# Roots and x2 loaded ahead of the first gathers, and a retimed steady schedule, in a one-core S5, conformer and PEER step

## The chip, the cores and the metric

One NeuronCore of a Trainium2 chip runs the whole kernel. The metric is the device time of the kernel in microseconds (us). Its engines are TensorE (PE), VectorE (DVE), ScalarE (ACT), GpSimd (POOL) and SyncE (SP); SP, ACT and POOL also issue DMAs. "PEq", "ACTq", "SPq" and "POOLq" in the profile are the sequencers of these engines.

## The reference, cut to what matters

There are 1024 prompt rows and 64 sample rows of width 1024, all in float32. Each row goes through a mixing layer and then through a PEER layer:

```python
def _layer(x, ...):
    xn = _rmsnorm(x, norm_mix)
    z = xn @ w_in                       # [u_ssm 512 | conv GLU input 1024 | gates 2048]
    y_ssm = S5(u_ssm)                   # diagonal complex state space
    branch_a = pa * sigmoid(qa)         # pa, qa = gelu(y_ssm) @ w_ssm_glu
    v = p * sigmoid(q)                  # conv GLU
    out = causal_depthwise_conv(v, width 31) + conv_b
    branch_b = silu(layernorm(out)) @ w_conv_out
    x = x + (sigmoid(g_A) * branch_a + sigmoid(g_B) * branch_b) @ w_out      # "x2"
    return x + peer(_rmsnorm(x, norm_ffn))

def block(xb):                          # PEER, 128 rows at a time
    q = (xb @ w_q).reshape(128, 8, 2, 128)
    v1, i1 = top_k(q[:, :, 0] @ keys1.T, 16);  v2, i2 = top_k(q[:, :, 1] @ keys2.T, 16)
    sc, pos = top_k(all sums v1 + v2, 16);     eidx = i1 * 128 + i2 at pos
    g = softmax(sc)
    act = gelu(sum(u_tab[eidx] * xb))   # one dot product per chosen expert
    return sum((g * act) * v_tab[eidx]) # 8 heads * 16 experts = 128 experts per row
```

A final RMSNorm follows. Every row picks its own 128 experts, so 8 KB (a row of u and of v) are fetched for each of 1088 x 128 choices: 1.14 GB.

## The kernel before, in words

**Two streams of work share the core.** The expert stream handles one tile of 128 rows at a time, 32 slots for each pair of heads. A slot is one gather of 128 expert rows (1 MB) into one of 8 ring buffers `rows` (POOL, line 1521), a dot product on DVE (line 1375), Gelu and the scaling of a diagonal matrix on ACT (lines 915 to 922), and two float32 products on PE that add the v rows into PSUM (line 760), after which the buffer is free again (`slot_free`). There are 1088 slots in 272 turns of 4 slots, so 64 turns for each group of two tiles. POOL issues the gathers of two turns ahead, as fast as buffers come free.

The mixing stream computes everything up to the scores of the PEER keys for one group of 272 rows (256 prompt, 16 sample) at a time; there are 4 groups. Its work is written out in half turns in two tables: `OPENING` for group 0 and `STEADY` for groups 1 to 3. The first dictionary of a table is the order of PE, the second that of the other engines; an entry `"cout": [68, 70, 72, 74]` puts the four pieces of this name into half turns 68, 70, 72 and 74. In `STEADY` ACT follows PE by one half turn (`lag` 1) where a piece is read from PSUM bank pair `ps_a`. The first `OPEN` (59) half turns of group 0 run alone. Then the turn loop starts. Turn t holds the half turns numbered 2t and 2t+1 of the mixing stream, called by `beside(number)`: on PE `beside(2t)`, two slots, `beside(2t+1)`, two slots. `mix_half` maps the number: the first 2 x `SKEW` (8) numbers finish group 0, and then 128 half turns of group 1 follow, and so on. So half turn 0 of a steady group lies at turns 4, 68 and 132, and half turn h lies h/2 turns behind it.

**The pieces that the change moves.** `xn` is 24 transposes on PE into 8 tiles of `ps_a` (2 banks), each copied out by ACT (`to_channels`, lines 599 and 800). `cq` is the first product behind it. `tap` is a unit of the depthwise convolution on DVE, four scalar_tensor_tensor instructions (line 1225); there are 32 units, the second 16 of them in half turns 31 to 46. `mean`, `centre`, `square`, `var`, `eps`, `root`, `scale` and `swish` are the layer norm behind the taps. `gate`, `glu`, `cout`, `out`, `q` are products of PE with 16 matmuls each (`out` has 6 more, which add x), and each reads one 512 KB slab of weights that SP loads into a ring of 4. `cout` on DVE (lines 1291 to 1296) forms `merged`, and PE's first `out` waits for all 8 of its parts (`merged_done`). `score` (line 698) goes to DRAM in `keep_scores` (ACT, lines 834 and 835) and `rows` (line 744) transposes x2 back into rows.

**Around the first gathers.** Each engine is an in-order queue. ACT stores x2 rows (`sq`, half turn 54) and inverse roots (`rs`, half turn 56) to DRAM. SP loads the scores of two heads back in half turns 54 and 56 (line 452), and in half turn 58 the x2 rows and the roots of tile 0 (`load_rows`, lines 461 and 462). DVE chooses the experts of the first pair behind its last opening half turn (`choose`, lines 1319 to 1351): `choose(0, 0)` and `choose(0, 1)` are the two key tops of head 0, `choose(0, 3)` gives its indices, on which POOL's first gather waits. ACT's `exps(0)` behind the opening needs the roots, DVE's `start(0)` (line 1389) needs x2 and roots, and each dot product comes after both.

## Time and profile before

| | us |
|---|---|
| median of 3 runs | 3489.51 |
| lowest, highest | 3487.99, 3494.52 |
| the profiled execution | 3491.98 |
| its span (first to last instruction) | 3489.9 |
| PE busy | 3148.8 (90%) |
| DVE busy | 2409.2 (69%) |
| POOL busy | 1417.6 (41%) |
| ACT busy | 1214.4 (35%) |

The span and all rows below are of the profiled execution. "DMA share" is the mean busy share of the 16 DMA engines in a stretch; it reads up to 1.02 where they never rest. A row of a timeline begins with start and duration in us from the start of the span; what stands in brackets is the idle time of the engine before it and what ended it. Times of matmuls are modelled at their ends.

### The profile page before, as it was taken

To read this page: it belongs to the slowest core of one execution; us is meant where nothing else is said; L and a number is where in the kernel's file an instruction comes from. 1 tells how busy PE (TensorE), PEld (TensorE's weight loads), DVE (VectorE), ACT (ScalarE), POOL (GpSimd) and SP (SyncE) were. 2 spreads that over 40 slices of the span, in tenths; PEclk is the share of its full clock that TensorE was granted. 3 is DMA by queue.
4 is the path that set the end of the run, shared out by engine and by line. 5 is a ranking of instruction groups with operands and counts; after the bars stand their busy time and mean duration, and the time that the engine had idled before them with its cause. 6 is when DMAs were issued, how large, how long until landed. Compare 5 with 4: busy or idle time off the path is not lost.

```text
span 3489.9 us, 33576 instructions
## 1 busy us (share of the span) xinstructions
PE 3148.8 (90%) x10016; PEld 1794.4 (51%) x10016; DVE 2409.2 (69%) x5463; ACT 1214.4 (35%) x4060; POOL 1417.6 (41%) x1240
## 2 busy tenths in 40 slices
PE   7998999999999999999999999999999777777776
PEld 6776555555655455555655555555555222322222
DVE  7824599776656699776656699777656666676674
ACT  4222443343333334343333343333333333333332
POOL 1201455433334355443334355343333444444443
PEclk9999999999999999999999999999999999999999
DMA  4257999999999999999999999999999999999998
GB/s 134 96 175 275 380 381 410 418 419 419 418 398 412 395 386 407 418 410 418 416 398 415 393 385 406 419 415 419 418 406 405 420 420 420 402 420 408 419 398 344
DMA packets 232069, 1336.40 MB, mean 383 GB/s; under 512 B 27664, under 2 KB 49296, under 8 KB 92624
## 3 DMA queue, kind: packets, MB, share of 16 engines
q0 software_dynamic: 156672, 1140.92, 79.7%
q1 hardware_dynamic: 62992, 179.96, 13.9%
q10 hardware_dynamic: 12224, 13.38, 1.1%
q8 instruction: 80, 1.31, 0.1%
q14 instruction: 101, 0.83, 0.1%
HBM read 1310.93 MB, written 23.23 MB: 382 GB/s over the span
## 4 chain that ended last, share of the span: by engine, by line
PE 53%; DMA 25%; DVE 10%; issue 5%; ACT 5%; POOL 2%; SPq 0%; POOLq 0%; DVEq 0%; ACTq 0%
PE ps_acc L760 29%; DMA rows<-in_experts,idx 24%; PE ps_a L596 13%; DVE rows L1375 4%; PE ps_a L671 4%; PE ps_v L596 3%; POOL rows L1521 2%; DVE va L1225 1%; PE ps_a L698 1%; ACT coef L918 1%; ACT uy L817 1%; ACT diag L922 1%; PE ps_y L638 1%; PE ps_a L675 1%; PE ps_v L682 0%
## 5 line engine op out<-in xcount | busy, mean ns | idle before, releaser
L760 PE MATMUL ps_acc<-rows,diag 128*128 128x512 f32 x4352 | 2020.8, 613 | 282.4 <-ACT diag L922 279.7
L1521 POOL DMA_INDIRECT rows<-in_experts,idx x1088 | 1280.1, 1177 | 1788.5 <-PE ps_acc L760 1468.6
L1375 DVE CUSTOM_DVE_ANT_0 rows<-rows,xn 128x1024 f32<-128x1024 f32 x1088 | 1328.4, 1232 | 839.1 <-DMA rows<-in_experts,idx 832.3
L760 PEld LDWEIGHTS ps_acc<-rows,diag 128*128 128x128 f32 x4352 | 824.3, 195 | 1335.4 <-issue 865.1
L915 ACT ACTIVATE act_v<-dots 128x2 f32<-128x2 f32 x544 | 110.6, 203 | 1894.1 <-DVE dots L1375 1891.1
L922 ACT ACTIVATE diag<-pk,coef 128x128 f32<-128x128 f32 x1088 | 377.2, 394 | 17.7
L596 PE MATMUL ps_a<-xnT,ring 128*128 128x272 f32 x1536 | 370.3, 396 | 0.9 <-ACT xnT L805 0.7
L596 PEld LDWEIGHTS ps_a<-xnT,ring 128*128 128x128 f32 x1536 | 293.4, 192 | 91.8 <-issue 34.8
L918 ACT ACTIVATE coef<-act_v,soft 128x1 f32<-128x1 f32 x1088 | 261.4, 287 | 17.9
L596 PE MATMUL ps_a<-gates,ring 128*128 128x272 f32 x1024 | 247.5, 395 | 15.2 <-ACT sig L892 14.4
L1225 DVE SCALAR_TENSOR_TENSOR va<-va,pk 128x302 f32<-128x302 f32 x480 | 250.2, 584 | 2.7
L596 PEld LDWEIGHTS ps_a<-gates,ring 128*128 128x128 f32 x1024 | 194.7, 191 | 78.2 <-issue 25.4
L671 PE MATMUL ps_a<-xnT,ring 128*128 128x272 f32 x512 | 130.3, 399 | 2.3 <-DVE xnT L1296 1.2
L596 PE MATMUL ps_v<-uy,ring 128*128 128x272 f32 x512 | 127.1, 398 | 2.5 <-ACT uy L873 2.5
L596 PEld LDWEIGHTS ps_v<-uy,ring 128*128 128x128 f32 x512 | 98.9, 193 | 28.6 <-issue 5.5
L671 PEld LDWEIGHTS ps_a<-xnT,ring 128*128 128x128 f32 x512 | 94.5, 190 | 31.1 <-issue 11.5
L1375 DVE DVE_READ_ACCUMULATOR2_ANT dots<- 128x1 f32 x1088 | 89.0, 82 | 0.0
L1493 POOL TENSOR_TENSOR rs<-rs,half 128x3 f32<-128x3 f32 x4 | 5.6, 1390 | 168.5 <-DVE rs L1172 168.4
L596 PE MATMUL ps_a<-uy,ring 128*128 128x272 f32 x256 | 65.9, 401 | 4.1 <-ACT uy L817 4.1
L596 PEld LDWEIGHTS ps_a<-uy,ring 128*128 128x128 f32 x256 | 49.6, 194 | 24.7 <-issue 11.5
L596 PE MATMUL ps_v<-xnT,ring 128*128 128x272 f32 x256 | 61.4, 393 | 0.0
L698 PE MATMUL ps_a<-pk,sig 128*128 128x128 f32 (+1 forms) x384 | 59.5, 275 | 0.0
(226 smaller groups left out, 2001.0 us busy)
## 6 DMA issues: line engine op xcount, KB each, us to landing
ring<-in_slabs SPq DMA_DIRECT2D x256, 512.0 KB, 7.8
rows<-in_experts,idx POOLq DMA_INDIRECT x1088, 12.6
ring<-made_slabs SPq DMA_DIRECT2D x24, 512.0 KB, 9.3
sc<-score_rows SPq DMA_DIRECT2D x68, 128.0 KB, 10.2
score_rows<-gp ACTq DMA_DIRECT2D x32, 256.0 KB, 9.6
xt<-in_x_prompt SPq DMA_DIRECT2D x4, 1024.0 KB, 13.1
x_rows<-xt ACTq DMA_DIRECT2D x4, 1024.0 KB, 12.3
x2t<-x_rows SPq DMA_DIRECT2D x8, 512.0 KB, 11.7
```

The source lines that it names most:

```text
L596: last = pe.matmul(out[:, 0:N], w, rhs[:, k, :], start=(k == 0), stop=(k == kt - 1))
L638: last = pe.matmul(out, w, hst[:, t % 2, c, i, 0:NK], start=False, stop=(c == 1))
L671: last = pe.matmul(out[:, 0:N], ring[:, slot, k * P:(k + 1) * P], merged[:, k, :], start=(k == 0), stop=(k == DT - 1))
L675: pe.matmul(out[:, n:n + width], xt[0:width, t, j * P:(j + 1) * P], eye2[0:width, 0:width], start=False, stop=False, skip_group_check=True)
L698: last = pe.matmul(out[0:width, t * KEYS:(t + 1) * KEYS], qT[:, m % 2, n:n + width], keys, start=True, stop=True)
L760: ins = pe.matmul(ps_acc[:, h, :], diag[:, slot, :], rows[:, slot, D + h * 512:D + (h + 1) * 512], start=first, stop=False, skip_group_che ...
L915: act.activation(act_v[:, cols], dots[:, cols], ACT.Gelu).then_inc(gelu_done, 1)
L918: act.activation(coef[:, s:s + 1], act_v[:, s:s + 1], ACT.Copy, scale=soft[:, n % 2, s:s + 1]).then_inc(coef_done, 1)
L922: act.activation(diag[:, s % RING, :], shape, ACT.Copy, scale=coef[:, s:s + 1]).then_inc(diag_done, 1)
L1225: last = dve.scalar_tensor_tensor(acc[:, c, :], src, wk, acc[:, c, :], ALU.mult, ALU.add)
L1375: ins = dve.tensor_tensor_reduce(rows[:, slot, 0:D], rows[:, slot, 0:D], xn[:, :], 1.0, 0.0, ALU.mult, ALU.add, dots[:, s:s + 1])
L1521: pool.indirect_dma_start(out=rows[:, slot, :], out_offset=None, in_=experts, in_offset=bass.IndirectOffsetOnAxis(ap=idx[:, a, k:k + 1], a ...
```

## The change

`OPEN` becomes 62 and `SKEW` 3: three more half turns of group 0 run ahead of the turn loop, two fewer lie inside it, and each steady group starts one turn earlier. In the opening SP loads scores one half turn earlier, x2 rows of tile 0 in half turn 55 and its roots in half turn 57, and DVE runs the first two `choose` steps at the head of its half turn 55, ahead of `ms2`. `xn` is cut into two parts of 4 tiles in half turns 0 and 1, and the first `cq` of a steady group goes from 1 to 2. Units 16 to 31 of the taps go to 31 + 3u/2 (31 to 53), the layer norm goes from 48..62 to 56..67, one gate from 54 to 69, `cout` on PE from 68..74 to 71..77 and on DVE from 70..76 to 73..79, and `out` from 77..91 to 78..92.

```diff
--- before.py
+++ after.py
@@ -64,7 +64,7 @@
 HALVES = 2 * TURNS
 PIECES = ("xn", "u", "cq", "cp", "s", "y", "gate", "glu", "mean", "var", "cout", "out", "rows", "q", "score")
 SLAB_OF = {"u": 0, "cq": S_CONV, "cp": S_CONV + 1, "gate": S_GATE, "glu": S_GLU, "cout": S_COUT, "out": S_OUT, "q": S_Q}
-A_TILES = {"xn": DT, "u": 1, "cq": 1, "gate": 1, "glu": 1, "out": 1, "q": 1, "score": 1}
+A_TILES = {"xn": DT // 2, "u": 1, "cq": 1, "gate": 1, "glu": 1, "out": 1, "q": 1, "score": 1}
 V_TILES = {"cp": 1, "s": 2, "glu": 1, "mean": 1, "var": 1, "cout": 2, "rows": 2}
 A_BANKS, V_BANKS = 2, 3
 
@@ -107,7 +107,7 @@
 
 
 OPENING = Plan(
-    {"xn": [0], "u": [1, 2, 3, 4], "cq": [5, 7, 9, 11], "cp": [6, 8, 10, 12],
+    {"xn": [0, 1], "u": [1, 2, 3, 4], "cq": [5, 7, 9, 11], "cp": [6, 8, 10, 12],
      "s": [10, 12, 14, 16], "y": [15, 18, 21, 24],
      "gate": [13 + m for m in range(13)] + [34 + m for m in range(3)], "glu": [26 + j for j in range(DT)],
      "mean": [29], "var": [32], "cout": [37, 38, 39, 40], "out": [42 + j for j in range(DT)],
@@ -120,27 +120,27 @@
      "cout": [38, 39, 40, 41], "rows": [52, 53, 54], "sq": [54], "ms2": [55], "rs": [56],
      "load_x": [59], "sq_next": [63], "ms_next": [64], "norm_next": [65]}, False, 0)
 STEADY = Plan(
-    {"xn": [0], "u": [9, 11, 21, 23], "cq": [1, 5, 13, 17], "cp": [3, 7, 15, 19],
+    {"xn": [0, 1], "u": [9, 11, 21, 23], "cq": [2, 5, 13, 17], "cp": [3, 7, 15, 19],
      "s": [12, 16, 24, 28], "y": [20, 24, 32, 36],
-     "gate": [25 + 2 * m for m in range(10)] + [44, 54] + [61 + 2 * m for m in range(4)],
+     "gate": [25 + 2 * m for m in range(10)] + [44] + [61 + 2 * m for m in range(5)],
      "glu": [45 + 2 * j for j in range(DT)],
-     "mean": [48], "var": [54], "cout": [68, 70, 72, 74], "out": [77 + 2 * j for j in range(DT)],
+     "mean": [56], "var": [61], "cout": [71, 73, 75, 77], "out": [78 + 2 * j for j in range(DT)],
      "rows": [94, 96, 98], "q": [93 + 2 * m for m in range(2 * HEADS)],
      "score": [95 + 2 * m for m in range(2 * HEADS)]},
     {"cp": [6, 10, 18, 22], "turn_in": [14, 18, 26, 30], "scan": [14, 18, 26, 30], "turn_back": [14, 18, 26, 30],
      "gelu": [21, 25, 33, 37],
-     "tap": [11, 12, 13, 15, 16, 17, 19, 20, 21, 22, 23, 24, 25, 27, 28, 29] + [31 + u for u in range(16)],
+     "tap": [11, 12, 13, 15, 16, 17, 19, 20, 21, 22, 23, 24, 25, 27, 28, 29] + [31 + 3 * u // 2 for u in range(16)],
      "glu": [48 + 2 * j for j in range(DT)],
-     "centre": [51], "square": [52], "eps": [57], "root": [58], "scale": [60], "swish": [62],
-     "cout": [70, 72, 74, 76], "rows": [96, 98, 100], "sq": [101], "ms2": [102], "rs": [104],
+     "centre": [58], "square": [59], "eps": [63], "root": [64], "scale": [66], "swish": [67],
+     "cout": [73, 75, 77, 79], "rows": [96, 98, 100], "sq": [101], "ms2": [102], "rs": [104],
      "load_x": [106], "sq_next": [117], "ms_next": [119], "norm_next": [121]}, True, 1)
 A_ALL, V_ALL = OPENING.a_all, OPENING.v_all
 
 SLABS_0, SLABS_G = len(OPENING.slabs), len(STEADY.slabs)
 SLABS = SLABS_0 + (GROUPS - 1) * SLABS_G
 
-SKEW = 4
-OPEN = 59
+SKEW = 3
+OPEN = 62
 ALL_TURNS = TILES * TPAIRS * PTURNS + SPAIRS * PTURNS
 LAST_PAIR = TILES * TPAIRS + SPAIRS - 1
 
@@ -459,6 +459,8 @@
             def load_rows(t):
                 rows_free(t)
                 sp.dma_start(x2t[:, t % 2, :], x2_t[t]).then_inc(x2_in, 16)
+
+            def load_roots(t):
                 sp.dma_start(rst[:, t % 2, :], rs_t[t]).then_inc(rs_in, 16)
 
             def beside(number):
@@ -496,13 +498,15 @@
                 mix(h, 0)
 
                 for b in range(2):
-                    if h == OPENING.pe["score"][2 * b + 1] + 2:
+                    if h == OPENING.pe["score"][2 * b + 1] + 1:
                         sp.wait_ge(score_out[b], 32)
                         load_scores(0, b)
-                if h == OPENING.pe["q"][8]:
+                if h == OPENING.other["ms2"][0]:
                     sp.wait_ge(rows_out, 32)
+                    load_rows(0)
+                if h == OPENING.other["rs"][0] + 1:
                     sp.wait_ge(rs_out, 48)
-                    load_rows(0)
+                    load_roots(0)
             sp.wait_ge(score_used, 1)
             sp.wait_ge(score_out[0], 64)
             load_scores(1, 0)
@@ -512,6 +516,7 @@
                 beside(2 * turn)
                 if k == 3 and g < GROUPS:
                     load_rows(2 * g + 1)
+                    load_roots(2 * g + 1)
                 if k == 1 and g < GROUPS:
                     sp.wait_ge(score_out[1], 128 * g + 64)
                     pass_wait()
@@ -529,6 +534,7 @@
                     sp.wait_ge(rs_out, 48 * (g + 2))
                     pass_wait()
                     load_rows(2 * g + 2)
+                    load_roots(2 * g + 2)
                 if turn == TILES * TPAIRS * PTURNS - 6:
                     rows_free(TILES)
                     for f in range(2):
@@ -596,15 +602,16 @@
                     last = pe.matmul(out[:, 0:N], w, rhs[:, k, :], start=(k == 0), stop=(k == kt - 1))
                 return last
 
-            def to_channels(n0, g):
+            def to_channels(n0, part, g):
 
                 pe.wait_ge(xh_ready, g + 1)
-                for k in range(DT):
-                    out = a_tile(n0 + k)
+                for k in range(DT // 2 * part, DT // 2 * (part + 1)):
+                    out = a_tile(n0 + k % (DT // 2))
                     for t in range(2):
                         pe.transpose(out[:, t * P:(t + 1) * P], xh[t][:, k * P:(k + 1) * P], eye)
                     pe.transpose(out[:, NP:N], xh[2][:, k * P:(k + 1) * P], eye[0:NS, 0:NS]).then_inc(a_ready, 1)
-                a_emptied(n0 + DT - 1)
+                if part == 1:
+                    a_emptied(n0 + DT // 2 - 1)
 
             def states(t, g):
 
@@ -701,8 +708,8 @@
 
             def mix(h, g):
                 at = plan(g).at
-                for _ in at("xn", h):
-                    to_channels(a_at(g, "xn"), g)
+                for part in at("xn", h):
+                    to_channels(a_at(g, "xn", part), part, g)
                 for m in at("u", h):
                     to_a("u", m, xnT[:, :, :], g)
                 for j in at("cq", h):
@@ -798,9 +805,9 @@
                 act.activation(va[:, D:2 * D], xt[:, 1, :], ACT.Square, accum_out=ssq[:, 1:2])
                 act.activation(xh[2], xt[0:NS, 2, :], ACT.Square, accum_out=ssq[0:NS, 2:3]).then_inc(sq_x, 1)
 
-            def to_channels(n0, name, g):
-                for k in range(DT):
-                    src, out = ready(n0 + k), by_step(xnT[:, k, :])
+            def to_channels(n0, part, name):
+                for k in range(DT // 2 * part, DT // 2 * (part + 1)):
+                    src, out = ready(n0 + k % (DT // 2)), by_step(xnT[:, k, :])
                     act.activation(out[:, :, 0:KP], in_time(src[:, 0:NP]), ACT.Copy, scale=par(name)[:, k:k + 1])
                     act.activation(out[:, :, KP:NK], in_time(src[:, NP:N]), ACT.Copy,
                                    scale=par(name)[:, k:k + 1]).then_inc(a_done, 1)
@@ -840,8 +847,8 @@
                 def at(piece, h):
                     return plan(g).at(piece, h - plan(g).lag)
 
-                for _ in plan(g).at("xn", h):
-                    to_channels(a_at(g, "xn"), "norm_mix", g)
+                for part in plan(g).at("xn", h):
+                    to_channels(a_at(g, "xn", part), part, "norm_mix")
                 for m in at("u", h):
                     cross(uS[:, m, :], ready(a_at(g, "u", m)), ACT.Copy, False).then_inc(a_done, 1)
                 for j in at("cq", h):
@@ -1417,8 +1424,11 @@
             for h in range(OPEN):
                 if h == OPENING.pe["s"][0]:
                     setup_lags()
+                if h == OPENING.other["ms2"][0]:
+                    for r in range(2):
+                        choose(0, r)
                 mix(h, 0)
-            for r in range(PTURNS):
+            for r in range(2, PTURNS):
                 choose(0, r)
             dve.wait_ge(norms_in, 16)
             for turn in range(ALL_TURNS):
```

## Rows read from the trace of the kernel before

**Rows 1.** The page: DMA queue of the gathers, packets, MB, share of 16 engines.

```profile
q0 software_dynamic: 156672, 1140.92, 79.7%
```

**Rows 2.** Busy times by stretch: stretch, length, engines, PEclk, DMA share, GB/s.

```profile
303.00:334.00 31.00, 16.63 (x67) 12.07 (x66) 18.73 (x55) 8.71 (x26) 8.15 (x8) 0.78 1.00 391
...
354.00:384.00 30.00, 30.00 (x112) 18.36 (x110) 17.71 (x37) 12.06 (x39) 15.71 (x10) 1.00 0.87 319
...
580.00:596.00 16.00, 16.00 (x70) 11.08 (x69) 15.69 (x37) 7.66 (x32) 8.46 (x9) 1.00 0.94 377
596.00:750.00 154.00, 153.81 (x497) 92.14 (x496) 121.94 (x281) 57.34 (x182) 60.57 (x52) 1.00 1.02 418
...
840.00:950.00 110.00, 107.42 (x350) 63.51 (x349) 67.98 (x154) 35.46 (x119) 42.95 (x38) 0.98 1.01 418
...
964.00:990.00 26.00, 26.00 (x93) 15.48 (x93) 16.25 (x39) 10.67 (x34) 10.55 (x10) 1.00 0.96 370
...
1160.00:1184.00 24.00, 23.27 (x66) 13.27 (x67) 11.83 (x32) 7.60 (x27) 5.90 (x6) 0.83 0.88 332
...
1930.00:1962.00 32.00, 29.36 (x88) 16.26 (x87) 16.69 (x39) 11.84 (x42) 7.84 (x8) 0.84 0.88 351
```

**Rows 3.** DMA issues of 240 to 303 us: size, median us to landing.

```profile
score_rows<-gp ACTq DMA_DIRECT2D x3, 16.0 KB, 4.7
```

**Rows 4.** Timeline of the first gathers, SP, ACT, DVE, POOL and PE.

```profile
278.71 0.48 ACTq L835 DMA_DIRECT2D score_rows<-gp  x1
...
287.36 0.45 SPq L452 DMA_DIRECT2D sc<-score_rows  x1
...
292.63 0.29 DVE L1319 MAX8 topv<-sc 128x8 f32<-128x128 f32 x1 [5.13 <-DMA sc<-score_rows]
...
292.89 0.19 ACT L886 ACTIVATE rs<-rs 128x3 f32<-128x3 f32 x1
...
296.43 0.43 DVE L1329 TENSOR_TENSOR hot<-topv 128x256 f32<-128x256 f32 x1
...
303.10 1.19 POOL L1521 DMA_INDIRECT rows<-in_experts,idx  x1 [14.64 <-DVE idx L1351]
...
322.43 0.30 ACT L904 ACTIVATE neg_top<-best,rst 128x2 f32<-128x2 f32 x1 [15.62 <-DMA rst<-inverse_roots]
...
325.25 5.51 PE L596 MATMUL ps_a<-gates,ring 128*128 128x272 f32 x16 [14.37 <-ACT sig L892]
...
331.45 7.13 PE L760 MATMUL ps_acc<-rows,diag 128*128 128x512 f32 x16
...
334.25 1.75 POOL L1521 DMA_INDIRECT rows<-in_experts,idx  x1 [20.87 <-PE ps_acc L760]
```

**Rows 5.** Timeline of PE, half turns 0 and 1 of group 2.

```profile
1153.95 0.38 PE L605 MATMUL ps_a<-pk,va 128*128 128x128 f32 x2
...
1162.54 6.47 PE L760 MATMUL ps_acc<-rows,diag 128*128 128x512 f32 x8 [0.73 <-ACT xnT L805]
1168.85 3.83 PE L596 MATMUL ps_a<-xnT,ring 128*128 128x272 f32 x16
```

**Rows 6.** Timeline of PE and DVE, half turns 76 to 79 of group 1.

```profile
839.98 0.19 DVE L1296 SCALAR_TENSOR_TENSOR xnT<-gates,rot 128x16 f32<-128x16 f32 x1
...
843.71 5.40 PE L760 MATMUL ps_acc<-rows,diag 128*128 128x512 f32 x8 [2.58 <-ACT diag L922]
848.94 0.62 PE L671 MATMUL ps_a<-xnT,ring 128*128 128x272 f32 x2
...
853.57 7.03 PE L760 MATMUL ps_acc<-rows,diag 128*128 128x512 f32 x16
```

**Rows 7.** Gathers from issue to landing, of 790 to 840, 860 to 940, 2440 to 2505.

```profile
DMA to landing us min/median/max: 11.8/14.7/16.3
...
DMA to landing us min/median/max: 9.1/11.1/13.5
...
DMA to landing us min/median/max: 10.5/12.5/14.8
```

## The prediction

> **What bounds the kernel now.** I read the page first. PE is busy for 90% of the span, which looks like the bound, but the gathers alone are 1140.92 MB [rows 1], and the second question is whether the DMA engines ever rest. The table of busy times by stretch answers it [rows 2]. From 303 us on, where the first gather goes out, the DMA share is 1.00 to 1.02 in most stretches, at some 418 GB/s, and in a few short ones it is 0.87 to 0.96. So the end is set by three things: when the gathers begin, how many bytes follow (the change keeps them), and how long the DMA engines rest after that. A full stretch reads 1.01 or more, so rest is length x (1.01 - share): 30 x 0.14 = 4.2 us at 354 to 384 (end of the opening inside the turns), 16 x 0.07 = 1.1 at 580 to 596 (half turns 30 and 31), 26 x 0.05 = 1.3 at 964 to 990 (the `rows` and first `q` pieces), 24 x 0.13 = 3.1 at 1160 to 1184 (`xn` of group 2), 32 x 0.13 = 4.2 at 1930 to 1962 (`xn` of group 3). PE's load matters where it holds buffers back so long that the gathers' queue runs dry. How near that is, the issue-to-landing times tell: a median of 14.7 us at 790 to 840, but 11.1 at 860 to 940 [rows 7], where `out` runs. There PE never waits from 848.94 on, with one product and 4 slots each turn, and DMA is just full [rows 2, 6]. Third, the timelines of the first gathers and of the places that the change touches [rows 4 to 6].
>
> **The opening, start of the gathers.** The first gather (303.10) waits for the chain: scores stored (issue 278.71, some 4.7 us to land [rows 3], so 283.4), loaded (issue 287.36), first key top at 292.63, and 10.5 us of choosing [rows 4]. The load sits behind half turn 54 of SP. Moved one half turn up, it goes out when the store has landed, 283.4, which is 4.0 us earlier. `ms2` now stands between the key tops and the pair top: +0.2. First gather: 3.8 us earlier, at 299.3. Bounds: nothing, and the 4.6 us of a half turn.
> There is a new wait here: `ms2`, and behind it POOL's root and ACT's `rs`, come after the first scores have landed. The key tops take 296.43 - 292.63 = 3.8 us; from 288.6 they end at 292.4, the root a little later, while ACT stands at its `rs` at 292.89 [rows 4]: a wait of some 1 us. ACT owes PE its next copy only at the end of the product in work, so this costs nothing; if the scores land 3 us later, PE stands for the difference, still ahead of the gathers.
> By the Trainium skill ("DMA: Bandwidth & Descriptors", section on queues, rings and completion order) each DMA engine takes turns between the queues that have work, packet by packet. The store of x2 rows would then be in flight beside the earlier load of scores and take its share of it: the start would gain some 3 us instead of 3.8. No run here shows it yet.
>
> **The opening, bytes and refill.** The x2 load (0.52 MB, 1.2 us at 418 GB/s) now lies ahead of the gathers, where DMA has room: -1.2. PE is 3.8 of 4.6 us less far when they begin, so 0.8 of a 0.52 MB slab comes later: +1.0. The roots, issued behind 5 gathers and x2 before, ended a wait of 15.62 us on ACT at 322.43, and PE stood 14.37 us until 325.25 [rows 4]. That stall hid beside full DMA (share 1.00 at 303 to 334 [rows 2]), so its 14 us are not the gain. After: the roots go out near 301 and land in time, but ACT's `exps(0)` now stands behind half turn 61. PE was ready for half turn 60 at 325.25 - 14.37 = 310.9. A `q` with its `score` has 22 matmuls, as an `out` has, which takes 853.57 - 848.94 = 4.6 us [rows 6]; with that for each of 60 to 63 slots begin at 329.5 instead of 331.45, and the first refill at 332.3 instead of 334.25. The first 8 gathers, started 3.8 us earlier and with 3 slabs more beside them, last to about 331.7. So the queue is thin there: +1.0 (0 to 3).
>
> **The opening inside the turns.** Before, the products of half turns 61 to 65 lie between slots; two products and 4 slots are 9.3 + 7.0 = 16.3 us for a turn, against 11.5 us that DMA needs for 4 gathers and a slab. That is the rest of 4.2 us at 354 to 384. After, only 64 and 65 remain (62 and 63 come before the first slot, at turn 0): -4.2 (-2 to -4.3). Sum of the opening: -3.8 - 1.2 + 1.0 + 1.0 - 4.2 = -7.2, between -3 and -10.
>
> **`xn` in two parts.** In group 2 the block takes 1162.54 - 1153.95 = 8.6 us, at the end of which PEclk has fallen (0.83 over the stretch), and the two slots behind it take 6.47 us instead of 3.5 [rows 2, 5]. Two parts of 4.3 with slots between would save the 3.0 of the slow clock, if it stays high; but each part can wait for ACT, whose batch comes first, and all of it plus `cq` and `cp` still falls into two turns. Per group between 0 and the whole rest of 3.1 or 4.2; I take half of the clock's price, 1.5, for groups 2 and 3. Group 1 has no rest there to lose. Sum -3.0.
>
> **Taps and layer norm.** Half turns 32 to 53 lie in 596 to 750, where DMA is at 1.02 [rows 2]. DVE has less in each half turn, and DMA gets nothing from that: 0. The 1.1 us at half turns 30 and 31 come before the taps thin out (31 and 32 stay): -0.1 for each group, -0.3. Bounds -1.5 and +1.5, as the choosing steps beside the taps shift by one turn.
>
> **The products behind the layer norm.** This is what the change costs. Before, from half turn 77 to 93 PE has 8 `out` and one `q`; the last `cout` is at 74. After, `cout` at 77 is followed by `out` at 78, and `out` at 92 by `q` at 93: one product more (3.83 us, as [rows 5]) in a stretch in which PE never waits and after which DMA already rests (1.3 us at 964 to 990). The half turn that is relieved of a gate, 54, lies in the full stretch and gives nothing back. So the product goes to the end: +3.8 for group 1, the same for group 2; for group 3 the landings take 12.5 instead of 11.1 us [rows 7], so 1.4 is covered: +2.4. Sum +10.0. Bounds: 0, if PE can catch up, and 3 x 3.8 = 11.5.
> The new wait: PE's `out` at 78 needs the last merge, which DVE does in 79. Now the merge of half turn 76 ends at 839.98, and `out` of 77 begins at 848.94, 9.0 us later [rows 6]. The distance shrinks by two half turns, 11.5 us, so PE would wait 2.5; but PE also has the `cout` of 77 (3.83) ahead of it: 0 to 2.5, I take 0.5, three times: +1.5. Behind it stand the slots, then `slot_free`, then POOL's gathers.
>
> **Sum.** -7.2 - 3.0 - 0.3 + 10.0 + 1.5 = +1.0 on the profiled execution of 3491.98, so 3493. That execution is 2.5 above the median of the runs, so in their terms 3490.5: no change.
>
> **Rivals.**
> Faster (A): the extra product is absorbed. For it: over 790 to 840 the landing time has 3.6 us of reserve against 860 to 940 [rows 7], and PE waits before the stretch (2.58 us at 843.71 [rows 6]). Against: before the change the reserve is used up as well. Then -7.2 - 3.0 - 0.3 = -10.5, and if `xn` gives all of its 7.3, -14.8: 3475 to 3479, say 3478.
> Slower (B): PE's first `out` waits for the merge for long. DVE's merge of 79 stands behind two more dots, which wait for landings (1.05 MB at 418 GB/s, 2.5 us each), and the merging itself, so up to 7 us behind the dots of the half turn before. If PE waits 4 us and its clock drops so that two slots take 6.47 instead of 3.5, that is 7 for each group where nothing covers it; with 3.5 to 4 counted, 3 x 4 = 12 - 1.5 on top of the forecast: 3501. It decides from a wait of some 2 us on. Against: the merge is now 9 us early.
> The opening does not do what it says (C): x2 and roots are early, but `exps(0)` behind 61 holds the dots until 323 to 325 as before and DMA runs dry ahead of the refill. The opening then gives 3 instead of 7.2: 3494.5.
>
> **How the numbers follow.** A measurement of this kernel can tell about 0.2%, 7 us, from no change. Forecast 0.41 (its own range 3484 to 3497), A 0.34, B 0.14, C 0.11. Faster by over 7 us (under 3482.5): nearly all of A and 0.03 of the forecast, 0.35. Slower (over 3496.5): B, 0.03 of the forecast and 0.03 of C, 0.20. Same: 0.45. The range goes from the middle of A's span down a little, 3474, to the middle of B, 3503.
>
> **What would show it.** The first gather near 299 and PE without a gap of 14 us: the opening's start; the share of the 30 us behind turn 1 near 1.01: its end. The two slots behind `xn` at 3.5 us and the share around it above 0.95: the split. A share of 0.85 or so for some 26 us around the `rows` pieces, or a short dip at half turn 78, in all three groups: the extra product. A PE wait released by DVE at the first `out` (line 671), with its length: B. I am wrong if the share stays at 1.01 through half turns 77 to 100 (then it is A), or if DMA rests over 3 us between 325 and 335 (then C).

## The result, and the profile after

The changed kernel takes 3468.75 us (median of 5 runs, 3463.84 to 3475.66), the kernel before beside it 3490.52 (5 runs, 3487.99 to 3494.52). The ratio is 0.9936 [0.9923, 0.995]: 21.8 us or 0.6% faster. The forecast was no change (3490.5, range 3474 to 3503); the time lies below the range, and below what rival A gave (3478). The profiled execution took 3467.05, its span 3464.9.

The page after: span, the gathers' queue, and the groups of the slots (L767, before L760), of the gate products (L602, before L596) and of `out` (L678, before L671); a group's row ends with the idle time before it and what ended most of it.

```profile
span 3464.9 us, 33601 instructions
...
q0 software_dynamic: 156672, 1140.92, 80.1%
...
L767 PE MATMUL ps_acc<-rows,diag 128*128 128x512 f32 x4352 | 2011.8, 611 | 276.7 <-ACT diag L929 268.1
...
L602 PE MATMUL ps_a<-gates,ring 128*128 128x272 f32 x1024 | 246.3, 394 | 0.9 <-ACT gates L885 0.9
...
L678 PE MATMUL ps_a<-xnT,ring 128*128 128x272 f32 x512 | 130.6, 400 | 5.8 <-DVE xnT L1303 4.7
```

Packets and bytes of the gathers are those of [rows 1], and their share rose only because the span is shorter. The idle time of 0.9 us in the gates' row says that the stall of 14.4 us at half turn 60 [rows 4] is gone. The row of `out` shows the new wait.

Next the busy times by stretch, as [rows 2]. The stretches follow the work, so they lie 6 us earlier than before at first and up to 20 later on.

```profile
297.00:334.00 37.00, 37.00 (x166) 27.68 (x165) 14.83 (x42) 15.98 (x46) 9.26 (x10) 1.00 0.98 382
354.00:384.00 30.00, 28.87 (x98) 16.02 (x97) 18.36 (x39) 13.88 (x49) 11.98 (x11) 1.00 1.02 418
...
591.00:745.00 154.00, 147.61 (x457) 86.00 (x456) 121.66 (x285) 54.92 (x182) 61.96 (x55) 1.00 1.02 419
835.00:945.00 110.00, 110.00 (x372) 66.16 (x371) 71.06 (x161) 36.59 (x124) 44.77 (x38) 1.00 1.01 413
959.00:985.00 26.00, 26.00 (x88) 14.94 (x87) 14.34 (x35) 14.32 (x40) 9.76 (x9) 1.00 1.01 418
```

The end of the opening (354 to 384) went from 0.87 to 1.02. The stretch of `out` stayed at 1.01, and 959 to 985, where the extra product was to be paid, reads 1.01 against 0.96. That is what the prediction named as the sign of rival A.

To place the rest, I worked out length x (1.0155 - share) between the same gathers of each kernel, with unrounded shares (1.0155 is what the long full stretches read). The columns e1 to e7 are experiments of the next section. In us:

| | before | after | e1 | e2 | e4 | e7 |
|---|---|---|---|---|---|---|
| first gather goes out at | 303.1 | 297.3 | 298.2 | 304.6 | 292.9 | 298.3 |
| gathers 8 to 24: end of the opening, `xn` of group 1 | 4.5 | -0.2 | 2.4 | 4.4 | -0.1 | -0.2 |
| `xn` of groups 2, 3 | 3.6, 4.5 | 2.1, 2.0 | 3.6, 6.2 | 1.3, 0.8 | 2.0, 2.3 | 2.2, 0.0 |
| half turns 8 to 32 of groups 1, 2, 3 | 6.4, 5.3, 5.4 | 6.3, 2.6, 2.4 | 4.7, 4.6, 4.4 | 6.7, 7.1, 6.1 | 3.3, 4.6, 2.4 | 6.8, 5.8, 5.8 |
| `out` to `q` of groups 1, 2, 3 | 1.4, 0.9, 0.0 | 0.6, 0.9, 0.8 | 0.7, 0.3, 0.0 | 0.5, 0.7, 0.2 | 0.7, 0.5, 0.2 | 1.9, 1.1, 0.9 |
| all rest from the first to the last gather | 41.2 | 26.0 | 37.4 | 37.8 | 26.5 | 32.9 |

From before to after: the start -5.8, the end of the opening -4.7, `xn` -4.0, the half turns 8 to 32 -5.8, `out` and `q` 0.0. These are 20.3 of the 24.9 us between the two profiled executions. Of the other 4.6, 1.0 is rest behind group 3 (8.8 before, 7.8 after), and some 3.5 are no rest but shorter busy time of the DMA engines for nearly the same bytes, which I can't explain. One execution of each stands behind the table; an entry moves by up to 3 us between kernels that are the same there (after and e4 have 6.3 and 3.3 in half turns 8 to 32 of group 1).

**The start.** Timeline of the changed kernel from the store of the first scores to the refill: SP, ACT, DVE, POOL and PE.

```profile
278.48 0.48 ACTq L842 DMA_DIRECT2D score_rows<-gp  x1
...
282.67 0.33 SPq L452 DMA_DIRECT2D sc<-score_rows  x1
...
286.79 0.30 DVE L1326 MAX8 topv<-sc 128x8 f32<-128x128 f32 x1 [7.48 <-DMA sc<-score_rows]
...
290.59 0.17 DVE L1179 TENSOR_SCALAR rs<-ssq 128x3 f32<-128x3 f32 x1
...
292.66 0.19 ACT L893 ACTIVATE rs<-rs 128x3 f32<-128x3 f32 x1
...
293.40 0.43 SPq L461 DMA_DIRECT2D x2t<-x_rows  x1
...
297.33 1.19 POOL L1531 DMA_INDIRECT rows<-in_experts,idx  x1 [5.51 <-DVE idx L1358]
...
302.02 0.33 SPq L464 DMA_DIRECT2D rst<-inverse_roots  x1
...
320.44 0.28 ACT L911 ACTIVATE neg_top<-best,rst 128x2 f32<-128x2 f32 x1
...
329.10 7.13 PE L767 MATMUL ps_acc<-rows,diag 128*128 128x512 f32 x16
...
331.90 0.94 POOL L1531 DMA_INDIRECT rows<-in_experts,idx  x1 [24.50 <-PE ps_acc L767]
```

The store is at 278.48 (278.71 in [rows 4]), the load goes out at 282.67 instead of 287.36, and its data are there 4.1 us later instead of 5.3. From the first key top to the first gather there are 10.5 us in both. The two gains, 4.7 and 1.1, are the 5.8 within rounding. ACT has no wait at `rs`, and PE reaches its slots 2.4 us earlier than in [rows 4].

**`xn`.** Timeline of PE in the changed kernel, half turns 0 and 1 of group 2.

```profile
1129.74 0.38 PE L611 MATMUL ps_a<-pk,va 128*128 128x128 f32 x2
...
1133.59 0.54 PE L611 MATMUL ps_a<-pk,va 128*128 128x128 f32 x2 [2.77 <-ACT xnT L812]
...
1135.11 6.41 PE L767 MATMUL ps_acc<-rows,diag 128*128 128x512 f32 x8
1141.36 0.38 PE L611 MATMUL ps_a<-pk,va 128*128 128x128 f32 x2
...
1144.49 3.70 PE L767 MATMUL ps_acc<-rows,diag 128*128 128x512 f32 x8 [0.73 <-ACT xnT L812]
```

The prediction expected two slots at full speed behind the split. They are not: two slots still take 6.41 us (6.47 in [rows 5]). The first part holds a wait of 2.77 us for ACT, and behind it the granted clock is 0.53 of full speed, nearly all of it the lower of its two levels (1.2 instead of 2.4 GHz), as the busy times of these stretches show:

```profile
1129.00:1134.00 5.00, 2.23 (x11) 1.02 (x9) 3.77 (x7) 2.37 (x9) 2.68 (x2) 0.98 1.01 416
1134.00:1141.00 7.00, 7.00 (x13) 3.20 (x13) 5.25 (x11) 2.72 (x10) 0.99 (x1) 0.53 1.02 427
1141.00:1150.00 9.00, 8.07 (x31) 4.63 (x30) 6.06 (x16) 4.98 (x18) 2.87 (x3) 1.00 0.89 338
```

The slow slots merely stand between the parts now. Yet the rest of the DMA engines became shorter. What changed beside it stands in POOL's queue, first before, then after:

```profile
1154.93 0.94 POOL L1521 DMA_INDIRECT rows<-in_experts,idx  x1 [0.78 <-PE ps_acc L760]
1167.13 1.18 POOL L1521 DMA_INDIRECT rows<-in_experts,idx  x1 [11.27 <-PE ps_acc L760]
```

```profile
1130.72 1.62 POOL L1531 DMA_INDIRECT rows<-in_experts,idx  x1 [0.66 <-issue]
1139.70 0.99 POOL L1531 DMA_INDIRECT rows<-in_experts,idx  x1 [7.36 <-PE ps_acc L767]
```

The longest time in which no gather goes out fell from 12.2 to 9.0 us (in group 3 from 11.9 to 9.1). In these two kernels PE's own time did not change: it spends 5.4 + 3.1 = 8.5 us on the parts against 8.6. What the DMA engines notice is then the longest gap between two freed buffers. The other traces agree. Over the stretches of `xn` in groups 2 and 3, the eight kernels with the undivided `xn` have longest gaps of 11.0 to 13.3 us and 2.7 to 6.2 us of rest, the six with the divided one 5.7 to 9.7 and 0 to 2.3. No run changed the gap alone.

### The profile page after: what moved, and what is told of

It is laid out like the page before. It is cut to its first block, busy times and chain, and to the rows that moved or that the text cites. A ratio compares the mean times of both kernels' runs of the same rounds, so it can differ in the third digit from the quotient of the medians.

```text
span 3464.9 us, 33601 instructions
## 1 busy us (share of the span) xinstructions
PE 3138.7 (91%) x10016; PEld 1789.8 (52%) x10016; DVE 2402.5 (69%) x5463; ACT 1216.9 (35%) x4060; POOL 1414.5 (41%) x1240
## 4 chain that ended last, share of the span: by engine, by line
PE 52%; DMA 26%; DVE 10%; issue 6%; ACT 4%; POOL 2%; SPq 0%; POOLq 0%; DVEq 0%; ACTq 0%
PE ps_acc L767 29%; DMA rows<-in_experts,idx 24%; PE ps_a L602 13%; DVE rows L1382 4%; PE ps_a L678 4%; PE ps_v L602 3%; POOL rows L1531 2%; DMA sc<-score_rows 2%; DVE va L1232 2%; PE ps_a L705 1%; ACT coef L925 1%; ACT diag L929 1%; PE ps_a L682 1%; PE ps_y L645 1%; ACT uy L824 1%
## 5 line engine op out<-in xcount | busy, mean ns | idle before, releaser
L767 PE MATMUL ps_acc<-rows,diag 128*128 128x512 f32 x4352 | 2011.8, 611 | 276.7 <-ACT diag L929 268.1
L767 PEld LDWEIGHTS ps_acc<-rows,diag 128*128 128x128 f32 x4352 | 821.6, 194 | 1325.1 <-issue 861.9
L602 PE MATMUL ps_a<-xnT,ring 128*128 128x272 f32 x1536 | 370.0, 395 | 0.9 <-ACT xnT L812 0.7
L602 PEld LDWEIGHTS ps_a<-xnT,ring 128*128 128x128 f32 x1536 | 293.1, 192 | 91.1 <-issue 34.2
L602 PE MATMUL ps_a<-gates,ring 128*128 128x272 f32 x1024 | 246.3, 394 | 0.9 <-ACT gates L885 0.9
L602 PEld LDWEIGHTS ps_a<-gates,ring 128*128 128x128 f32 x1024 | 193.4, 190 | 62.5 <-issue 23.9
L678 PE MATMUL ps_a<-xnT,ring 128*128 128x272 f32 x512 | 130.6, 400 | 5.8 <-DVE xnT L1303 4.7
L602 PE MATMUL ps_v<-uy,ring 128*128 128x272 f32 x512 | 127.0, 398 | 2.5 <-ACT uy L880 2.5
L602 PEld LDWEIGHTS ps_v<-uy,ring 128*128 128x128 f32 x512 | 98.9, 193 | 28.5 <-issue 5.7
L678 PEld LDWEIGHTS ps_a<-xnT,ring 128*128 128x128 f32 x512 | 94.2, 190 | 35.5 <-issue 10.0
L602 PE MATMUL ps_a<-uy,ring 128*128 128x272 f32 x256 | 65.9, 401 | 4.1 <-ACT uy L824 4.1
L602 PEld LDWEIGHTS ps_a<-uy,ring 128*128 128x128 f32 x256 | 49.6, 194 | 24.7 <-issue 11.5
L1326 DVE MAX8 topv<-sc 128x8 f32<-128x128 f32 x136 | 39.4, 290 | 32.9 <-DMA sc<-score_rows 32.9
L602 PE MATMUL ps_v<-xnT,ring 128*128 128x272 f32 x256 | 61.4, 393 | 0.0
## 6 DMA issues: line engine op xcount, KB each, us to landing
x2t<-x_rows SPq DMA_DIRECT2D x8, 512.0 KB, 11.1
```

Source lines behind the costliest of these rows:

```text
L602: last = pe.matmul(out[:, 0:N], w, rhs[:, k, :], start=(k == 0), stop=(k == kt - 1))
L678: last = pe.matmul(out[:, 0:N], ring[:, slot, k * P:(k + 1) * P], merged[:, k, :], start=(k == 0), stop=(k == DT - 1))
L767: ins = pe.matmul(ps_acc[:, h, :], diag[:, slot, :], rows[:, slot, D + h * 512:D + (h + 1) * 512], start=first, stop=False, skip_group_che ...
L1326: step(dve.max(topv[:, f, 0:8], s))
```

## The experiments

Each was measured in 5 to 12 executions. Their base is the kernel before or after, as told. Beside them the kernel before measured 3490.35 (e1 to e4), 3492.95 (e5 to e8) and 3490.49 (e9 to e12). A ratio is to the kernel before; what stands in brackets behind it is its 95% interval, in which 0.001 is 3.5 us.

**e1: the opening alone** on the kernel before.

```diff
-SKEW = 4
-OPEN = 59
+SKEW = 3
+OPEN = 62
+ (the hunks of load_rows, load_roots, load_scores and choose)
```

> The kernel before with the opening of the change alone: OPEN 62, SKEW 3, x2 rows and roots loaded ahead, the two key tops ahead of ms2. xn, taps, layer norm and products stay as before. Measured for the whole change: 21.8 us. Theory 1 (the opening gives its start and the rest at 354 to 384 us, and nothing in the steady groups): 11 us faster. Theory 2 (the shift of the steady groups by one turn also moves the taps against the choosing steps, and that is where the DMA rest of half turns 12 to 31 in groups 2 and 3 fell by some 6 us): 16 to 17 us faster, with less rest there. My forecast on record had 7 us for this part.

Measured: 3481.53, ratio 0.9976 [0.9963, 0.999], 8.8 us faster; single runs from 3473.93 to 3492.17. The predicted 7.2 holds as a sum, and the 16 to 17 us of theory 2 do not.

**e2: `xn` in two parts alone** on the kernel before.

```diff
-"xn": [0] ... "cq": [1, 5, 13, 17]
+"xn": [0, 1] ... "cq": [2, 5, 13, 17]
+ (A_TILES and to_channels as in the change)
```

> The kernel before with xn in two parts and the first cq of a steady group in half turn 2, nothing else. Theory 1 (only the rest behind xn falls): 3 to 4 us faster. Rival (a PE that is less late behind xn also helps the half turns 12 to 18, whose rest fell in groups 2 and 3): 8 to 10 us faster. If each part waits for ACT and the clock still falls: no change.

Measured: 3483.14, 0.9978 [0.9968, 0.9987], 7.2 us faster: more than twice the predicted 3.0, and near the whole rest of 3.1 + 4.2 that stood there. Here the clock's price did fall: in group 2 the two slots behind the first part take 5.40 us (6.47 in [rows 5]) and the parts 4.2 + 3.1 = 7.3 instead of 8.6.

**e3: the tables alone** (taps, layer norm, gate, `cout`, `out`) on the kernel before.

```diff
-"mean": [48], "var": [54], "cout": [68, 70, 72, 74], "out": [77 + 2 * j ...]
+"mean": [56], "var": [61], "cout": [71, 73, 75, 77], "out": [78 + 2 * j ...]
+ (and the other entries of STEADY, but for xn and the first cq)
```

> The kernel before with the steady tables alone: second half of the taps over 31 to 53, layer norm, one gate, cout and out later. Opening and xn as before. My forecast on record says 10 to 11 us slower, all of it DMA rest around half turns 78 to 98, by the product that comes to the end of the stretch in which PE never waits. Theory 1 (the product is covered, since PE and its clock no longer drop ahead of the first out): no change, within 3 us. Rival (thinner taps help): 3 to 6 us faster.

Measured: 3492.57, 1.001 [1.0001, 1.0019], 2.2 us slower by the medians and 3.5 by the ratio. The prediction had 11.2 for these edits. Row of `out` on the page of the kernel before, then on that of e3:

```profile
L671 PE MATMUL ps_a<-xnT,ring 128*128 128x272 f32 x512 | 130.3, 399 | 2.3 <-DVE xnT L1296 1.2
```

```profile
L671 PE MATMUL ps_a<-xnT,ring 128*128 128x272 f32 x512 | 132.3, 404 | 7.2 <-DVE xnT L1296 6.2
```

The new wait is (7.2 - 2.3) / 3 = 1.6 us for each group in e3, and (5.8 - 2.3) / 3 = 1.2 after.

**e4: the change without these tables**, the converse.

```diff
 (the changed kernel)
-"tap": ... + [31 + 3 * u // 2 for u in range(16)]
+"tap": ... + [31 + u for u in range(16)]
+ (and the other entries of e3 as before the change)
```

> The changed kernel with its steady tables (taps, layer norm, gate, cout, out) put back as before; opening and split xn stay. By my forecast on record this would be 10 us faster than the changed kernel (some 3459 us). Theory 1 (tables give nothing): as the changed kernel, 3469. Rival (the tables carry the gain of the tap half turns): 3475.

Measured: 3470.25, 0.9943 [0.9929, 0.9956], against 0.9936 [0.9923, 0.995] of the changed kernel. The tables cost nothing that can be told apart on the changed kernel; the 10 us of the forecast would have shown.

**e5, e6: one product, and three, more in the stretch of `out`** of each steady group, on the kernel before. They test the step "nothing covers it" by itself.

```diff
+                if g and h in (86,):            # e6: (82, 86, 90)
+                    for k in range(DT):
+                        pe.matmul(ps_y[:, 0:N], mean_w[:, :], merged[:, k, :], start=(k == 0), stop=(k == DT - 1))
```

> The kernel before with one more product of 8 float32 products (3.8 us of PE, no slab, result not used) in half turn 86 of each steady group, in the middle of the out pieces: the cost in dispute by itself. As the prediction on record has it (nothing covers PE there): 3 x 3.8 = 11 us slower. Theory 1 (the gathers in flight cover it, and PE catches up behind half turn 100): under 3 us.

> The same with three more products in each steady group, in half turns 82, 86 and 90: 11.4 us of PE for each group. No cover: 34 us slower. If the cover is one product for each group: 23 us slower. If PE's load here did not matter at all: no change. Together with the run with one product it gives the size of the cover.

Each such product holds PE for 3.83 us ([rows 5] has the same form). e5 adds 11.5 and measured 3495.93, 1.0011 [1.0002, 1.002]: +3.8 (0.7 to 7.0 by the interval). e6 adds 34.5 and measured 3520.42, 1.0076 [1.0063, 1.0089]: +26.5 (22.0 to 31.1). What did not arrive is 7.7 and 8.0 us, 2.6 and 2.7 for each group. Two runs fit a cover of a fixed size, after which each microsecond of PE is one of the kernel: from e5 to e6 the kernel grows by 22.7 us for 23.0 of PE. By the intervals the cover is 1 to 4 us for each group. Not all of it is rest of the DMA engines: of the 29.9 us between the profiled executions of the kernel before and e6, 15 are rest between `out` and `q`, and some 14 are longer busy time of the DMA engines for the same bytes. Busy times by stretch of e6, group 1, and landings of the gathers, e6 over 900 to 1010 us and after it the changed kernel over 850 to 930, its own stretch of `out`:

```profile
851.00:900.00 49.00, 49.00 (x168) 30.40 (x167) 32.15 (x77) 17.73 (x60) 17.79 (x16) 1.00 0.99 396
900.00:950.00 50.00, 50.00 (x177) 32.13 (x176) 26.07 (x61) 14.28 (x48) 14.14 (x15) 1.00 0.96 363
950.00:1000.00 50.00, 50.00 (x177) 29.60 (x176) 30.91 (x68) 14.85 (x52) 20.71 (x17) 1.00 0.95 377
```

```profile
DMA to landing us min/median/max: 5.9/8.2/15.1
```

```profile
DMA to landing us min/median/max: 9.0/10.6/13.7
```

When DMA does rest, at 0.95 to 0.96, the median gather lands in 8.2 us. The 11.1 of [rows 7] was thus not an empty reserve: 11.1 - 8.2 = 2.9 us were left, near the 2.6. In group 3 of the changed kernel (2420 to 2485) the median was even 9.7 us, with the share still at 1.01.

**e7: the changed kernel with its steady groups one turn later.**

```diff
-SKEW = 3
+SKEW = 4
 OPEN = 62
```

> The changed kernel with SKEW 4 in place of 3 and OPEN 62 as it is: opening, split xn and tables of the change, but each steady group starts one turn later, where it was before (turns 4, 68, 132). The runs so far have 6.1 us of DMA rest in half turns 8 to 32 of a group where SKEW is 4 (before, and the runs with xn or tables alone), and 3.9 where it is 3. Theory 2 (the alignment of the taps with the choosing steps sets this rest): 6 us slower than the changed kernel, some 3475, rest back at 6 a group. Theory 1 (it was chance): as the changed kernel, within 3 us.

Measured: 3475.45, 0.9954 [0.9941, 0.9966]: 6 us slower than the changed kernel by the ratios (4 by the medians, each against its own runs of the kernel before), though their intervals overlap between 0.9941 and 0.995. The opening is as after. In the traces the loss stands in half turns 8 to 32: 18.4 us of rest in the three groups against 11.3 (busy times by stretch of e7, then of the changed kernel, groups 2 and 3, the same gathers):

```profile
1224.00:1405.00 181.00, 169.19 (x595) 102.29 (x594) 164.50 (x353) 70.34 (x260) 97.48 (x89) 0.98 0.98 395
...
1997.00:2177.00 180.00, 170.19 (x594) 102.56 (x593) 159.57 (x352) 70.11 (x259) 96.92 (x89) 0.97 0.98 397
```

```profile
1227.00:1398.00 171.00, 160.07 (x569) 96.78 (x568) 148.32 (x338) 70.44 (x260) 88.97 (x81) 0.99 1.00 405
...
1999.00:2169.00 170.00, 161.51 (x569) 97.56 (x568) 148.97 (x338) 70.43 (x260) 89.75 (x80) 0.98 1.00 405
```

**e8: the loads and the early `choose` only**, `SKEW` 4 and `OPEN` 59 kept. **e9: `SKEW` 3 and `OPEN` 62 only.** Both on the kernel before; together they are e1.

```diff
 # e8
+ (the hunks of load_rows, load_roots, load_scores and choose)
```

```diff
 # e9
-SKEW = 4
-OPEN = 59
+SKEW = 3
+OPEN = 62
```

> The kernel before with the loads alone: scores one half turn earlier, x2 rows and roots ahead of the first gathers, two key tops ahead of ms2; OPEN 59 and SKEW 4 stay. If the early start and the early roots are the gain of the opening: 8 us faster (start 4, x2 1, and dots that begin near 306 in place of 325 take the rest of 4.5 us at 354 to 384). If three half turns of products out of the first turns are the gain: 4 us faster, by the start alone, and the rest at 354 to 384 stays.

> The kernel before with OPEN 62 and SKEW 3 alone; loads, choosing order, xn and tables as before. Starts the gathers as before (24.4 us behind the store of the first scores; 18.9 with the loads). By the alignment (rest of half turns 8 to 32 down by some 2 us a group, measured 6 us in all by the run one turn late) and three half turns fewer beside the first slots: 5 to 8 us faster. If the roots, which here still land behind the gathers, hold the dots until 322 us and the longer lone opening then delays the first refill: no change.

Measured: e8 3486.18, 0.9981 [0.9971, 0.9991], -6.6 by the ratio; e9 3487.15, 0.999 [0.9981, 1.0], -3.5. Their sum of 10.1 is e1's 8.8 within the spread. Which part is the larger can't be told: their intervals overlap. Neither removes the rest at the end of the opening by itself. From gather 8 to 48 it is 5.2 us in e8 and 5.6 in e9 (4.6 before, 2.9 in e1), so neither of e8's two theories is borne out in full: the time came near the 8 us of the first, but the rest of 4.5 us that was to pay for part of it stayed.

**e10: the products behind the layer norm alone** on the kernel before (gate 54 to 69, `cout` and `out` later; taps and layer norm as they were).

```diff
-"gate": ... + [44, 54] + ..., "cout": [68, 70, 72, 74], "out": [77 + 2 * j ...]
+"gate": ... + [44] + ..., "cout": [71, 73, 75, 77], "out": [78 + 2 * j ...]
-"cout": [70, 72, 74, 76]
+"cout": [73, 75, 77, 79]
```

> The kernel before with gate, cout and out later (one product more in half turns 77 to 93), taps and layer norm as before. The runs with extra products cost 3.8 and 26.5 us for 11.4 and 34 us of PE, so a cover of 2.5 us for each group. By that: 3 x (3.8 - 2.5) = 4 us slower. By the prediction on record: 10 to 11 us slower. If a product moved is cheaper than a product added, since PE and its clock do not drop ahead of the first out: no change.

Measured: 3495.19, 1.001 [1.0001, 1.0019], +3.5 (0.3 to 6.6 by the interval). The cover of 2.6 gives 3 x (3.83 - 2.6) = 3.7. As e3, with the taps spread as well, has the same ratio, the spreading by itself does nothing that can be told apart, as predicted. The traces agree on the size: from `out` to `q` the six kernels with the moved product (after, e3, e7, e10 to e12) have 1.8 to 5.0 us of rest in the three groups, the six with neither a moved nor an added one 0.7 to 2.3, so some 2 us more in the mean.

**e11, e12: the changed kernel two turns later, and one turn earlier.**

```diff
 # e11
-SKEW = 3
+SKEW = 5
 # e12
-SKEW = 3
-OPEN = 62
+SKEW = 2
+OPEN = 63
```

> The changed kernel with SKEW 5 and OPEN 62: the steady groups two turns later than in the change. One turn later cost 6 us, all of it DMA rest in half turns 8 to 32. If the alignment with the choosing steps sets that rest, it is another value again here, not the same 6.1 us a group by rule; if what matters is only that the groups end earlier or later, it is 6 us slower again than one turn late, 3481.

> The changed kernel with SKEW 2 and OPEN 63: the steady groups one turn earlier than in the change, one more half turn of the opening alone. A candidate for a faster kernel: if earlier is better by rule, 6 us faster than the change, 3463; if it is the alignment, the rest of half turns 8 to 32 may go either way; the longer lone opening delays the first refill by up to 4.6 us.

Measured: e11 3472.86, 0.995 [0.9937, 0.9962]; e12 3472.61, 0.9948 [0.9935, 0.9961]. Neither beats the changed kernel. The rest in half turns 8 to 32 was 2.6, 1.9, 6.3 in e11 and 4.6, 6.2, 4.5 in e12. e12 also pays at the start: with one half turn more ahead of the slots the queue runs dry before the refill.

```profile
333.00:345.00 12.00, 9.27 (x28) 6.34 (x29) 3.71 (x13) 6.95 (x19) 0.00 (x0) 0.72 0.57 210
```

The changed kernel has 0.98 over its 37 us there, so with one half turn less in the opening the queue just lasts.

## Why the prediction was wrong

**The step that failed** is "So the product goes to the end: +3.8 for group 1, the same for group 2", with "nothing covers it": +10.0, and +1.5 for the wait. It made a gain into no change. On the kernel before, these edits cost 3.5 (e3 and e10, by the ratio), on the changed one nothing that can be told apart (e4). "DMA is just full" was read as "the reserve is gone"; e5 and e6 show 2.6 us of it in each group. A landing time of 11.1 us says little as long as one does not know what it is when the queue does run dry (8.2).

It is not the whole miss. Forecast and result lie 22.8 us apart. By the medians 12.9 of them are the tables (+11.2 in the sum, -1.7 from e4 to the changed kernel; 7.7 if e3 is taken), 4.2 `xn`, 1.6 the opening, and 4.1 what opening and `xn` bring together. The second step that failed is the 0 for the shift of the steady groups, below.

**The new wait** was there, 1.2 us for each group (1.6 in e3 and e10), within its range of 0 to 2.5. The product alone is more than the cover, so by the same sum the wait should have added 3 x 1.6 = 4.8 us to e3 and e10. Their 3.5 leaves little room for it, and why it is not seen stays open. Rival B's wait of 4 us did not come.

**The opening's start**: -5.8 against -3.8. The load went out 4.7 us earlier, a whole half turn of SP, because the store had landed 4.2 us after its issue, half a microsecond sooner than the median of [rows 3]; and the load itself took 1.1 us less. By the Trainium skill ("DMA: Bandwidth & Descriptors", section on queues, rings and completion order) each DMA engine takes turns between the queues that have work, which was to cost part of this gain; here the earlier load was the faster one (landed 4.0 us after its issue, 5.1 before), so the trace shows nothing of such a loss. It does not refute the rule: both loads had other transfers beside them, the later one the store of the next scores at 288.32. The wait of ACT at `rs` did not come: the root was ready in time. Against the store, the start is 18.9 us after it instead of 24.4.

**The refill**: PE came to its slots 2.4 us earlier (1.9 predicted), the first refill at 331.90 (332.3 predicted), and DMA ran at 0.98 up to there: +1.0 allowed for, 37 x 0.03 = 1.1 read. Rival C is out.

**The opening inside the turns**: -4.7 against -4.2, right in size partly by luck, since the step had only half of its cause. e1 removes 2.1 of it and e2 nothing; only both together remove all. In this stretch lies `xn` of group 1 too, of which the prediction said that it "has no rest there to lose". In e1 (first fence) the undivided `xn` at 362 leaves 24 us at 0.91; in the changed kernel (second) the 20 us are full:

```profile
360.00:384.00 24.00, 22.67 (x69) 11.97 (x68) 13.40 (x29) 9.96 (x35) 6.88 (x7) 0.86 0.91 355
```

```profile
360.00:380.00 20.00, 18.87 (x66) 10.46 (x65) 13.21 (x29) 9.35 (x33) 7.11 (x6) 1.00 1.02 420
```

That fits with opening and `xn` together bringing 20.1 us (e4) and only 8.8 + 7.2 = 16.0 apart, though by the intervals the 4.1 us between the two are within the spread; the traces put 2.6 of them here.

**`xn`**: 7.2 by e2 against 3.0. The bound "the whole rest" was right. The value taken was half the price of the slow clock, and that is not what the rest follows: in the changed kernel the clock fell as before and the rest still shrank by 1.5 and 2.5 us in groups 2 and 3. In e2, where PE gained 2.4 us in group 2, it shrank by 2.3 and 3.7.

**The half turns 8 to 32** had 0 in the sum, with a bound of -1.5 to +1.5 for all groups. The prediction counted 13.9 us of rest in the kernel before and left out 16 of the 17 us that stand here in the three groups. One dip of group 1 among them, busy times by stretch:

```profile
476.00:512.00 36.00, 35.39 (x135) 22.12 (x134) 35.20 (x81) 9.07 (x34) 21.69 (x21) 1.00 0.87 331
```

The shift of the steady groups by one turn, which comes with `SKEW` 3, brought 5.8 in groups 2 and 3 by the traces and some 6 by e7. Over all kept traces it is clearer: in the three groups together the rest there is 15.7 to 19.9 us in the eight kernels with `SKEW` 4 and 10.3 to 13.8 in the four with 3, 5.5 apart in the mean. It does not go one way with the shift (10.9 in e11 with 5, 15.3 in e12 with 2). What it is in the position that matters stays open. Every pair of heads takes 8 turns of choosing on DVE, so a shift moves those steps against the taps; that these are the cause was only argued, and no run moved the one without the other. The 6 us by e7 are also near what a measurement can tell.

In short, by the experiments: opening -8.8, `xn` -7.2, the two together 4.1 more (within the spread), tables 0 to +3.5. With the full rest of `xn` and of the opening (3.1 + 4.2 + 4.2) and the cover, the prediction's own terms would have given -11.5 - 3.8 - 1.2 + 2.0 - 0.3 + 3 x (3.8 - 2.6) = -11.2, so 3478, the value of A, with the wait at nothing. The measured time is 9 us below even that. The rest that the shift removes could be seen before; which way a shift would move it could not.

## What to carry to other kernels

Where DMA sets the end, price a step by the longest time without a freed buffer and by how far the queue is from dry, not by PE's busy time; "share 1.01 and PE never waits" does not mean that the next product is paid in full. Find the size of that reserve by adding one and then three units of harmless work: here two runs gave 2.6 and 2.7 us, each with an interval of 1 us or more to either side. Two edits that each shorten a stop in the same stretch are to be summed only after looking whether both stops lie under one dip of the DMA share.

## What the runs showed of the hardware

- Gathers land in 9.7 to 14.7 us (medians of stretches) while the DMA share is 1.01 to 1.02, and in 8.2 us at a share of 0.96 (e6, 900 to 1010 us). The landing time is a gauge of the queue's depth: it falls before the share does.
- Kernels with the same opening differ, one execution of each, by up to 5 us ahead of the first scores, before anything that the change touches: the first gather was at 297.3 in the changed kernel and at 292.9 in e4. A difference of that size at the start of one trace means nothing, unless it is taken from the store of the scores on.
- In the changed kernel a wait of PE of 2.77 us among the small transposes of `xn` was followed by a granted clock of 0.53 (near its lower level, 1.2 GHz) over 7 us, and two slots then took 6.41 instead of 3.70 us. In e7 the wait in the same place was 1.71 us, and the two slots took 5.40. With the transposes undivided the clock also fell where the longest wait among them was 0.20 us (e1, group 1: 0.86 over 360 to 384 us).
